# Products of gathered rows taken earlier and in smaller lots in the expert search of a two-part transformer block, with fewer early weight chunks

## The chip, the cores and the metric

The kernel runs on 1 core of one Trainium2 chip. The metric is device time in microseconds (us) of one execution, median over the runs shown.

## The reference, cut to what matters

One sequence of 256 tokens with 1024 features goes through a first block (block attention, difference attention, then an expert layer) and a second block (two attention mixers). The change lies in the expert layer:

```python
def chunk_fn(xc):                                   # 128 tokens at a time
    q = (xc @ w_query).reshape(C, PEER_HEADS, 2, PEER_HALF)
    sc = jnp.einsum('thpd,hpnd->thpn', q, sub_keys)
    top_s, top_i = lax.top_k(sc, PEER_TOPK)         # 16 of 128, for 8 heads x 2 halves
    cand_s = top_s[:, :, 0, :, None] + top_s[:, :, 1, None, :]
    best_s, best_pos = lax.top_k(cand_s, PEER_TOPK) # 16 pairs a head: 128 slots a token
    experts = jnp.take_along_axis(cand_i, best_pos, axis=-1)
    gates = jax.nn.softmax(best_s, axis=-1)
    u, vv = expert_down[experts], expert_up[experts]
    act = jax.nn.gelu(jnp.einsum('cd,chkd->chk', xc, u), approximate=False)
    return jnp.einsum('chk,chkd->cd', gates * act, vv)
```

There are 16,384 experts, each with a row of 1024 numbers in `expert_down` and one in `expert_up`.

## The kernel before, in words

The function select_phase does everything of the expert layer up to the weights of the experts; experts_phase then multiplies these with `expert_up`. The 256 tokens are two tiles of 128, called t = 0 and t = 1 here, and the two are treated differently:

- **Tile 1** is multiplied with all of `expert_down`. Its 128 chunks of 128 experts (512 KB each) are loaded by SyncE (Chunks.load, L1314 and L1317), TensorE multiplies one (Chunks.project, L1331, 16 matmul records a chunk), and ScalarE takes the gelu of four chunks at a time (Chunks.gelu, L1342).
- **Tile 0** gathers only the rows it chose. For each of the 128 slots GpSimd issues one indirect DMA of one row a token (512 KB, L1459) and VectorE multiplies and sums that buffer in one instruction (the function dots, L1682). There are GATHERS = 12 gather buffers; gather s waits until product s - 12 is done (semaphore `dotted`).

Both kinds of load use the same 16 DMA engines, through two queues: SyncE's and GpSimd's.

The order in which the stages come, on the engines:

1. **Queries and scores.** 16 half heads hp. For each, SyncE loads a 576 KB piece of weights (`route`, L1426, into ring buffer hp % 4 once the scores of hp - 4 are out), ScalarE and GpSimd split it (L1542, L1450), TensorE makes the queries (L245 to L247) and the scores (L1487). Behind each of the 12 loads of this stage SyncE puts one load of an early chunk; the other early chunks go out before the first of them. EARLY = 18 chunks are early: they lie where table and gather buffers lie later, 12 of them in the 12 gather buffers, so the first 12 gathers wait for TensorE to be through with them (`projected`). The later chunks use a ring of 6 buffers.
2. **The searches** on VectorE. halves(t, h) finds the 16 best scores of both halves of one head (L1611, L1614, L1616), pairs(t, n) the best sums of four heads (L1631 and the same top-16 rows), indices(t, n) their numbers (L1646 to L1664), choose(n) hands 64 slots of tile 0 to GpSimd (L1675). TensorE works through AHEAD = 56 chunks meanwhile. ScalarE puts the exp of the gates (L1571) behind the gelu of 48 chunks and ahead of the rest.
3. **The slot transposes** (L1493) and then **the table of tile 1**, 16 groups of 8 tokens: VectorE makes one one-hot factor (onehots, L1703), ScalarE the other (equal, L1553 and L1556), TensorE multiplies them (spread, L1505), ScalarE copies one part out (L1581), VectorE merges the other (merge, L1716). Between the groups TensorE has the chunks up to 80, and VectorE DOTS_GROUP = 3 products a group, 17 times.
4. **The rest**: the other chunks up to 120 on TensorE, the other products and the joins (join, L1724) on VectorE, all paced so that the last product and the last of these chunks end together.
5. **The table of tile 0**, 16 groups, which needs all products of tile 0; then the expert phase.

The constants `DOTS_...` say how many products VectorE has done where: 4 after the second choose, 1 after each of the last four halves of tile 1, 3 after each indices of tile 1, 2 before the slot transposes: 16 before the table, 67 behind it.

```python
for n in range(2):
    for h in range(4 * n, 4 * n + 4):
        halves(0, h)
        if n == 0:
            halves(1, h)
    pairs(0, n); indices(0, n); choose(n)
```

Of the kernel before, what the change touches and what calls it, by code (L numbers as in the profile page):

```python
# [32 lines left out]
NT = SEQ // P  # L33
# [8 lines left out]
HEADS_P = 8  # L42
TOPK = 16
SLOTS = HEADS_P * TOPK
# [2 lines left out]
FIRST_FREE = 4  # L47
UP_RING = 4
GATHERS = 12
EARLY = GATHERS + 6  # L50
EARLY_ROWS = 2
BEFORE = 48
AHEAD = 56
BESIDE = 32
TAIL = 8
WAITING = BESIDE // 4
DOTS_FIRST, DOTS_HALVES, DOTS_INDEX, DOTS_TURN, DOTS_GROUP = 4, 1, 3, 2, 3
RECTANGLES = ((0, 0, 1, 16), (16, 1, 4, 8), (40, 4, 8, 4), (56, 8, 16, 1))
PAIRS = 64
BY_SCALAR = (0, 1, 2, 5, 8, 11, 14)  # L60
# [1284 lines left out]
def select_phase(nc, d, hT, hT_at, whole, sbt, raw, landed_q, table, table_at, h_row, chunks, gather_in, up_in):  # L1345
# [3 lines left out]
    HP = 2 * HEADS_P  # L1349
    NW = 4  # L1350
    Q = 8
    GROUPS = P // Q
    BATCH = 4
    BATCHES = GROUPS // BATCH
    begun = DOTS_FIRST + 4 * DOTS_HALVES + 2 * DOTS_INDEX + DOTS_TURN + DOTS_GROUP * (GROUPS + 1)
    last_groups = (NKEYS - TAIL - BEFORE - BESIDE) // 4
    beside = [AHEAD + (BEFORE + BESIDE - AHEAD) * g // GROUPS for g in range(GROUPS + 1)]
    COARSE = P // FINE
# [28 lines left out]
    with ExitStack() as c:  # L1387
# [28 lines left out]
        @block.sync  # L1416
        def _(sp):
            sp.dma_start(h_row[:], d["ffn_row"].broadcast_to([P, D])).then_inc(gain_in, 16)
            sp.dma_start(starts[:], d["c_starts"]).then_inc(starts_in, 16)
            sp.dma_start(mask_word[:], d["c_masks"]).then_inc(masks_in, 16)  # L1420
            first = EARLY - (HP - NW)
            for n in range(first):
                chunks.load(sp, n)
            for hp in range(NW, HP):
                sp.wait_ge(s_ready, hp - NW + 1)
                sp.dma_start(raw[hp % NW][:], weights[hp]).then_inc(landed_q[hp % NW], 16)  # L1426
                chunks.load(sp, first + hp - NW)
            for n in range(EARLY, NKEYS):
                if n < EARLY + RING - FIRST_FREE:
                    pass  # L1430
                elif n < EARLY + RING:
                    sp.wait_ge(s_ready, HP - NW + chunks.buffer(n) + 1)
                else:
                    sp.wait_ge(chunks.projected, n - RING + 1)
                paced = n // 4 - (BEFORE + BESIDE) // 4 - 1
                if paced > 0:
                    sp.wait_ge(dotted, begun + (SLOTS - begun) * min(paced, last_groups) // last_groups)
                chunks.load(sp, n)
            for n in range(UP_RING):
                sp.wait_ge(chunks.projected, chunks.last_in(n) + 1)  # L1440
                sp.dma_start(raw[n][:, 0:KD, :].rearrange("p k c -> p (k c)"), d["up"][n]).then_inc(up_in[n], 16)

        @block.gpsimd
        def _(pool):
            for hp in range(2, HP):
                b = hp % NW
                for h in range(2):
                    k = slice(KD // 2 * h, KD // 2 * (h + 1))
                    pool.wait_ge(w_highs, hp * 2 + (h - 3))
                    pool.tensor_tensor(w_low[b % 2][:, k], raw[b][:, k], w_high[b % 2][:, k].bitcast(F32),  # L1450
                                       ALU.subtract).then_inc(w_lows, 1)
            for s in range(SLOTS):
                if s % PART == 0:
                    pool.wait_ge(chosen, s // PART + 1)
                if s < GATHERS:
                    pool.wait_ge(chunks.projected, EARLY_ROWS + s + 1)
                else:
                    pool.wait_ge(dotted, s - GATHERS + 1)
                pool.indirect_dma_start(gathered[s % GATHERS], None, d["down_rows"],  # L1459
                                        bass.IndirectOffsetOnAxis(ap=expert[:, s:s + 1], axis=0)).then_inc(gather_in[s % GATHERS], 16)  # L1460
# [143 lines left out]
        def _(dve):  # L1604
# [14 lines left out]
            def halves(t, h):  # L1619

                dve.wait_ge(s_saved, 2 * h + 2)
                top16([(saved[:, hp, t * P:(t + 1) * P], rest[:, hp % 2, :], lambda r, hp=hp: topv[:, t, hp, 8 * r:8 * r + 8],
                        lambda r, hp=hp: topu[:, t, hp, 8 * r:8 * r + 8]) for hp in (2 * h, 2 * h + 1)])

            def pairs(t, n):

                first, second = [topv[:, t, n * HEADS_P + half:(n + 1) * HEADS_P:2, :] for half in range(2)]
                four = HEADS_P // 2
                for at, lo, hi, width in RECTANGLES:
                    shape = [P, four, hi - lo, width]  # L1630
                    dve.tensor_tensor(cand[:, :, at:at + (hi - lo) * width].rearrange("p i (a b) -> p i a b", b=width),  # L1631
                                      first[:, :, lo:hi].unsqueeze(3).broadcast_to(shape),
                                      second[:, :, 0:width].unsqueeze(2).broadcast_to(shape), ALU.add)
                dve.drain()
                top16([(cand[:, i], crest[:, i], lambda r, at=(n * four + i) * TOPK: bestv[:, t, at + 8 * r:at + 8 * r + 8],
                        lambda r, at=(n * four + i) * TOPK: pos[:, t, at + 8 * r:at + 8 * r + 8]) for i in range(four)])
# [37 lines left out]
                dve.drain()  # L1674
                dve.tensor_copy(expert[:, at], number[:, at]).then_inc(chosen, 1)  # L1675

            def dots(lo, hi):

                for s in range(lo, hi):
                    b = s % GATHERS  # L1680
                    dve.wait_ge(gather_in[b], s // GATHERS * 16 + 16)
                    dve.tensor_tensor_reduce(gathered[b], gathered[b], h_row[:], 1.0, 0.0, ALU.mult, ALU.add, u[:, s:s + 1]).then_inc(dotted, 1)  # L1682

            def digit(t, n, part):

# [41 lines left out]
            dve.scalar_tensor_tensor(h_row[:], x[:, 0, :], sbt["root"][:, 0:1], h_row[:], ALU.mult, ALU.mult)  # L1727
            dve.wait_ge(starts_in, 16)
            dve.wait_ge(masks_in, 16)
            for n in range(2):  # L1730
                for h in range(4 * n, 4 * n + 4):
                    halves(0, h)
                    if n == 0:
                        halves(1, h)
                pairs(0, n)
                indices(0, n)
                choose(n)
            at = DOTS_FIRST
            dots(0, at)
            for n in range(2):  # L1740
                for h in range(4 * n, 4 * n + 4):
                    if n == 1:
                        halves(1, h)
                        dots(at, at + DOTS_HALVES)
                        at += DOTS_HALVES
                pairs(1, n)
                indices(1, n)
                dots(at, at + DOTS_INDEX)
                at += DOTS_INDEX
            for t in range(NT):  # L1750
                v = bestv[:, t, :].rearrange("p (h k) -> p h k", k=TOPK)
                last = dve.tensor_tensor(gate[:, t, :].rearrange("p (h k) -> p h k", k=TOPK), v,
# [16 lines left out]
                v = gate[:, t, :].rearrange("p (h k) -> p h k", k=TOPK)  # L1769
                last = dve.tensor_tensor(v, v, ginv[:, t, :].unsqueeze(2).broadcast_to([P, HEADS_P, TOPK]), ALU.mult)  # L1770
            last.then_inc(cols_ready, 1)
            dots(at, at + DOTS_TURN)
            at += DOTS_TURN
            dve.wait_ge(cols_turned, 2)
            dve.tensor_copy(slotT[:, 1], slots[:, 1])
            dve.tensor_copy(slotT[:, 0, 0:3], slots[:, 0, 0:3])
# [3 lines left out]
            for g in range(GROUPS + 1):  # L1780
                if g < GROUPS:
                    onehots(1, g)
                if g > 0:
                    merge(g - 1)
                dots(at, at + DOTS_GROUP)
                at += DOTS_GROUP
            first, last = BEFORE // 4, (NKEYS - TAIL) // 4
            middle = (BEFORE + BESIDE) // 4
            for g in range(first, middle):
                join(g, late_gelu[g - first])  # L1790
            left = SLOTS - at
            for n, g in enumerate(range(middle, last)):
                dots(at + left * n // (last - middle), at + left * (n + 1) // (last - middle))
                join(g, late_gelu[(g - first) % WAITING])
            dve.drain().then_inc(dots_done, 1)
            for part in range(2):
# [121 lines left out]
def build(nc, d, out):  # L1918
    ctx = ExitStack()
    with ctx:  # L1920
# [29 lines left out]
        with ExitStack() as c0:  # L1950
# [71 lines left out]
            with ExitStack() as c:  # L2022
                table_at = -(-nc.sbuf_base // 32) * 32
                table = sb("table", [P, NT, NKEYS, P], c=c)
                h_row = sb("h_row", [P, D], c=c)
                up_in = [sem(f"up_in{b}") for b in range(UP_RING)]
                with ExitStack() as c2:
                    in_ring, in_rows = [[table[:, t].rearrange("p n t -> p (n t)")[:, b * D:(b + 1) * D].rearrange("p (k e) -> p k e", k=KD)
                                         for b in range((GATHERS, EARLY - GATHERS)[t])] for t in range(NT)]
                    early = in_rows[0:EARLY_ROWS] + in_ring + in_rows[EARLY_ROWS:]  # L2030
                    chunks = Chunks(nc, c2, plain_u, d["downT"], whole, raw, early)
                    select_phase(nc, d, hT, hT_at, whole, sbt, raw, landed_q, table, table_at, h_row, chunks, gather_in, up_in)
                c1.close()
                cleared = experts_phase(nc, d["up"], table, hT, x, whole, raw, up_in, sbt["sums"], sbt["ident"])
# [82 lines left out]
```

## Time and profile before

| | before |
|---|---|
| median of 3 runs | 1519.17 us (1518.54 to 1522.5) |
| the profiled execution: its own time | 1524.2 us |
| the profiled execution: span from first to last instruction | 1522.4 us |
| TensorE busy | 1409.8 us (93%) |
| VectorE busy | 993.1 us (65%) |
| ScalarE busy | 636.8 us (42%) |
| GpSimd busy | 205.5 us (13%) |
| read from HBM | 304.73 MB |

Busy time is an average over stages with different limits: the stage that the change touches lies between 183 us and 627 us of the span. In the rows, PE is TensorE, DVE VectorE, ACT ScalarE, POOL GpSimd and SPq the DMA-issuing queue of SyncE. "table" in a row can be any of the things that lie in the table's memory: scores, search scratch, gather buffers, early chunks.

### The profile page before, as it was taken

The page shows a single profiled execution, that of the slowest core. Times are in us where ns is not written, and L with a number is a line of the kernel's source. Part 1 is how long each engine was busy: PE and PEld are TensorE (multiplying, and loading weights), DVE is VectorE, ACT ScalarE, POOL GpSimd, SP SyncE. Part 2 cuts the span into 40 slices and gives each one's busy share as a digit, 9 for nine tenths or more (in the row PEclk, how much of TensorE's full clock was granted, in tenths as well). Part 3 has the DMA queues.
Part 4 walks back from the last instruction along what each step waited for, and adds up shares of the span by engine and source line. Part 5 has one row for each costly group of instructions (what it writes and reads, how often), then busy time and mean ns, then how long its engine had stood idle before and what let it go on. Part 6 is the DMA issues. An engine that isn't in the chain of part 4 may idle for free. (4 is left out here: it accounts for less than half of the span.)

```text
span 1522.4 us, 24797 instructions
## 1 busy us (share of the span) xinstructions
PE 1409.8 (93%) x8327; PEld 1212.7 (80%) x8327; DVE 993.1 (65%) x2325; ACT 636.8 (42%) x1256; POOL 205.5 (13%) x170
## 2 busy tenths in 40 slices
PE   7998989997896758999999999999999999989998
PEld 4665689997796658777777777789999999659994
DVE  4666569977996567566666666665555555256761
ACT  2433242017750005433333333356665665326651
POOL 0000164325876420000000000000000000000000
PEclk9999999999997988999999999999999999999999
DMA  8330187898999992365656556485554443236630
GB/s 299 133 137 1 46 333 263 314 386 307 404 409 409 409 403 85 99 191 181 191 188 185 192 182 191 138 249 176 178 153 153 152 152 111 91 89 193 183 90 28
DMA packets 145527, 307.17 MB, mean 202 GB/s; under 512 B 39968, under 2 KB 89632, under 8 KB 143904
## 3 DMA queue, kind: packets, MB, share of 16 engines
q1 hardware_dynamic: 127008, 238.93, 46.9%
q0 software_dynamic: 18432, 67.12, 11.5%
q8 instruction: 50, 0.82, 0.2%
q14 instruction: 37, 0.30, 0.1%
HBM read 304.73 MB, written 1.29 MB: 201 GB/s over the span
## 5 line engine op out<-in xcount | busy, mean ns | idle before, releaser
L1331 PE MATMUL plain_u<-whole,ring 128*128 128x128 f32 x1760 | 218.3, 285 | 34.6 <-DMA ring<-in_downT 34.6
L1331 PEld LDWEIGHTS plain_u<-whole,ring 128*128 128x128 f32 x1760 | 210.8, 200 | 40.2 <-DMA ring<-in_downT 40.0
L1882 ACT ACTIVATE hT_high<-ring 128x1024 fp32r<-128x1024 f32 x128 | 135.8, 1061 | 224.8 <-PE experts_acc L247 223.7
L245 PE MATMUL experts_acc<-hT_high,experts_wh 128*128 128x512 f32 x512 | 204.5, 399 | 1.5 <-DVE hT_low L1898 1.5
L246 PE MATMUL experts_acc<-hT_low,experts_wh 128*128 128x512 f32 x512 | 203.2, 397 | 0.0
L247 PE MATMUL experts_acc<-hT_high,experts_wl 128*128 128x512 f32 x512 | 203.2, 397 | 0.0
L1682 DVE CUSTOM_DVE_ANT_0 table<-table,h_row 128x1024 f32<-128x1024 f32 x128 | 152.3, 1223 | 45.1 <-DMA table<-in_down_rows,select_expert 41.6
L1459 POOL DMA_INDIRECT table<-in_down_rows,select_expert x128 | 161.6, 1262 | 145.1 <-DVE select_u L1682 101.4
L1898 DVE TENSOR_TENSOR hT_low<-ring,hT_high 128x1024 fp32r<-128x1024 f32 x128 | 156.9, 1226 | 27.4 <-ACT hT_high L1882 27.4
L245 PE MATMUL mix_a_pj<-mix_a_wh,hT_high 128*128 128x384 f32 x368 | 129.1, 351 | 0.0
L245 PEld LDWEIGHTS experts_acc<-hT_high,experts_wh 128*128 128x128 f32 x512 | 96.6, 189 | 35.2 <-issue 7.5
L247 PE MATMUL mix_a_pj<-mix_a_wh,hT_low 128*128 128x384 f32 x368 | 123.5, 336 | 0.0
L246 PE MATMUL mix_a_pj<-mix_a_wl,hT_high 128*128 128x384 f32 x368 | 123.4, 335 | 0.0
L247 PEld LDWEIGHTS experts_acc<-hT_high,experts_wl 128*128 128x128 f32 x512 | 96.8, 189 | 23.3
L246 PEld LDWEIGHTS experts_acc<-hT_low,experts_wh 128*128 128x128 f32 x512 | 96.9, 189 | 17.8
L1342 ACT ACTIVATE table<-plain_u 128x512 f32<-128x512 f32 x30 | 17.9, 597 | 203.3 <-PE plain_u L1331 189.6
L675 PE MATMUL block_pj<-block_w_raw,whole 128*128 128x384 f32 x256 | 91.1, 487 | 1.0 <-PEq L1196 1.0
L624 DVE TENSOR_TENSOR mix_a_wl<-mix_raw,mix_a_wh 128x1536 fp32r<-128x1536 f32 x46 | 80.5, 1756 | 14.3 <-ACT mix_a_wh L855 12.5
L1894 DVE CAST experts_wh<-table 128x256 fp32r (+1 forms) x128 | 37.8, 295 | 75.1 <-PE experts_acc L247 74.8
L246 PEld LDWEIGHTS mix_a_pj<-mix_a_wl,hT_high 128*128 128x128 f32 x368 | 69.4, 188 | 0.0
L245 PEld LDWEIGHTS mix_a_pj<-mix_a_wh,hT_high 128*128 128x128 f32 x368 | 69.3, 188 | 0.0
L247 PEld LDWEIGHTS mix_a_pj<-mix_a_wh,hT_low 128*128 128x128 f32 x368 | 69.1, 188 | 0.0
(393 smaller groups left out, 2601.9 us busy)
## 6 DMA issues: line engine op xcount, KB each, us to landing
ring<-in_up SPq DMA_DIRECT2D x128, 512.0 KB, 3.5
ring<-in_downT SPq DMA_DIRECT2D x110, 512.0 KB
mix_raw<-in_wa SPq DMA_DIRECT2D x46, 768.0 KB, 6.2
block_w_raw<-in_w SPq DMA_DIRECT2D x16, 768.0 KB, 6.2
mix_raw<-in_wb SPq DMA_DIRECT2D x16, 768.0 KB, 6.7
ring<-in_route SPq DMA_DIRECT2D x16, 576.0 KB, 5.2
table<-in_downT SPq DMA_DIRECT2D x18, 512.0 KB, 6.0
wo<-in_wo SPq DMA_DIRECT2D x4, 1024.0 KB, 7.9
```

What stands on the lines that cost most here:

```text
L245: pe.matmul(out, lhs[0], rhs[0], start=start, stop=False, skip_group_check=True)
L246: pe.matmul(out, lhs[0], rhs[1], start=False, stop=False, skip_group_check=True)
L247: return pe.matmul(out, lhs[1], rhs[0], start=False, stop=stop, skip_group_check=True)
L624: eng.tensor_tensor(wl[w][:, k, c], pieces.raw[w][:, k, c], wh[w][:, k, c].bitcast(F32), ALU.subtract).then_inc(lows, 1)
L675: mm = pe.matmul(dst[:, 0:3 * P], hT[:, k, chunks[i][1] * P:(chunks[i][1] + 1) * P], pieces.raw[b][:, k, :], start=k == 0, stop=k == KD - ...
L1331: mm = pe.matmul(self.u[g % 2][:, i * P:(i + 1) * P], rows[:, k, :], self.h[:, k, P:SEQ], start=k == 0, stop=k == KD - 1, skip_group_check ...
L1342: act.activation(into, self.u[g % 2][:], ACT.Gelu).then_inc(self.taken, 1)
L1459: pool.indirect_dma_start(gathered[s % GATHERS], None, d["down_rows"], bass.IndirectOffsetOnAxis(ap=expert[:, s:s + 1], axis=0)).then_inc( ...
L1682: dve.tensor_tensor_reduce(gathered[b], gathered[b], h_row[:], 1.0, 0.0, ALU.mult, ALU.add, u[:, s:s + 1]).then_inc(dotted, 1)
L1882: act.activation(uh[b % 2], raw_u[b], ACT.Copy).then_inc(u_high, 1)
L1894: dve.tensor_copy(wh[b % 2][:], table[:, :, n, :])
L1898: dve.tensor_tensor(ul[b % 2], raw_u[b], uh[b % 2].bitcast(F32), ALU.subtract).then_inc(u_low, 1)
```

## The change

The first four gather buffers no longer hold early chunks, so there are 14 early chunks instead of 18; the first four gathers wait for `chosen` alone, and gathers 4 to 11 each for the chunk in their buffer. Products now begin inside the first search: 2 after each of the halves of heads 5, 6 and 7 of tile 0, 5 after each of three indices, 3 after each pairs of tile 1, 2 after each of the last four halves of tile 1, 3 before the slot transposes: 38 before the table instead of 16. In the table a group has 1 and 2 products in turn instead of 3: 25 instead of 51, so 63 are done behind the table instead of 67, and 65 instead of 61 remain. TensorE has 60 chunks before the slot transposes and 20 between the groups of the table, instead of 56 and 24.

```diff
-EARLY = GATHERS + 6
+FREE = 4
+EARLY = GATHERS - FREE + 6
-AHEAD = 56
+AHEAD = 60
-DOTS_FIRST, DOTS_HALVES, DOTS_INDEX, DOTS_TURN, DOTS_GROUP = 4, 1, 3, 2, 3
+DOTS_FIRST, DOTS_LISTS, DOTS_PAIRS, DOTS_INDEX, DOTS_TURN = 2, 2, 3, 5, 3
...
-            first = EARLY - (HP - NW)
+            first = max(0, EARLY - (HP - NW))
...
-                if s < GATHERS:
-                    pool.wait_ge(chunks.projected, EARLY_ROWS + s + 1)
-                else:
+                if FREE <= s < GATHERS:
+                    pool.wait_ge(chunks.projected, EARLY_ROWS + s - FREE + 1)
+                elif s >= GATHERS:
                     pool.wait_ge(dotted, s - GATHERS + 1)
...
+            for h in range(4):
+                halves(0, h)
+                halves(1, h)
+            pairs(0, 0)
+            indices(0, 0)
+            choose(0)
+            at = 0
+            for h in range(4, HEADS_P):
+                halves(0, h)
+                if h > 4:
+                    at = dots(at, DOTS_FIRST)
+            pairs(0, 1)
+            indices(0, 1)
+            choose(1)
+            at = dots(at, DOTS_INDEX)
+            pairs(1, 0)
+            at = dots(at, DOTS_PAIRS)
+            indices(1, 0)
+            at = dots(at, DOTS_INDEX)
+            for h in range(4, HEADS_P):
+                halves(1, h)
+                at = dots(at, DOTS_LISTS)
+            pairs(1, 1)
+            at = dots(at, DOTS_PAIRS)
+            indices(1, 1)
+            at = dots(at, DOTS_INDEX)
...
-            dots(at, at + DOTS_TURN)
-            at += DOTS_TURN
+            at = dots(at, DOTS_TURN)
...
-                dots(at, at + DOTS_GROUP)
-                at += DOTS_GROUP
+                at = dots(at, 1 + g % 2)
```

SyncE's queue at the start of the stage: `table<-in_downT` is an early chunk, `ring<-in_route` a weight piece. Before:

```order
L1418 DMA h_row<-in_ffn_row 128x1024
L1419 DMA select_starts<-in_c_starts 128x17
L1420 DMA select_mask_word<-in_c_masks 128x1
L1314 DMA table<-in_downT 128x1024 x6
L1426 DMA ring<-in_route 128x1152
```

Now:

```order
L1420 DMA h_row<-in_ffn_row 128x1024
L1421 DMA select_starts<-in_c_starts 128x17
L1422 DMA select_mask_word<-in_c_masks 128x1
L1316 DMA table<-in_downT 128x1024 x2
L1428 DMA ring<-in_route 128x1152
```

Two early chunks stand ahead of the first weight piece of this queue instead of six.

VectorE in the halves of heads 5 and 6 of tile 0, between the first choose and the second (an ISA row with `table,select_u<-table,h_row` is a product; the ISA row behind it reads its sum). Before:

```order
L1611 MAX table<-table 128x8 x2
L1614 MAX_INDEX table<-table 128x8 x2
L1611 MAX table<-table 128x8 x2
L1614 MAX_INDEX table<-table 128x8
L1616 MATCH_REPLACE table<-table 128x128
```

Now:

```order
L1614 MAX table<-table 128x8 x2
L1617 MAX_INDEX table<-table 128x8 x2
L1685 ISA table,select_u<-table,h_row 128x1024
L1685 ISA select_u 128x1
L1685 ISA table,select_u<-table,h_row 128x1024
L1685 ISA select_u 128x1
L1614 MAX table<-table 128x8 x2
```

Two products stand where head 6 followed on head 5.

VectorE in two groups of the table of tile 1. Before:

```order
L1703 TENSOR_TENSOR select_a_one_1992<-select_coarse_of,select_fine_of 128x1024
L1716 TENSOR_TENSOR table<-table,select_four 128x48x8
L1682 ISA table,select_u<-table,h_row 128x1024
L1682 ISA select_u 128x1
L1682 ISA table,select_u<-table,h_row 128x1024
L1682 ISA select_u 128x1
L1682 ISA table,select_u<-table,h_row 128x1024
L1682 ISA select_u 128x1
L1703 TENSOR_TENSOR select_a_one_1991<-select_coarse_of,select_fine_of 128x1024
```

Now:

```order
L1707 TENSOR_TENSOR select_a_one_1992<-select_coarse_of,select_fine_of 128x1024
L1720 TENSOR_TENSOR table<-table,select_four 128x48x8
L1685 ISA table,select_u<-table,h_row 128x1024
L1685 ISA select_u 128x1
L1685 ISA table,select_u<-table,h_row 128x1024
L1685 ISA select_u 128x1
L1707 TENSOR_TENSOR select_a_one_1991<-select_coarse_of,select_fine_of 128x1024
```

One product fewer stands between these two one-hot factors; the group behind has one product where it had three.

## Rows read from the trace of the kernel before

**Rows 1.** The page's DMA issues: loads of ring chunks, with KB each
```profile
ring<-in_downT SPq DMA_DIRECT2D x110, 512.0 KB
```

**Rows 2.** Stretches: busy PE, PEld, DVE, ACT, POOL; clock; DMA share; GB/s
```profile
244.00:264.00 20.00, 20.00 (x179) 20.00 (x180) 18.24 (x111) 3.19 (x5) 7.67 (x8) 1.00 0.66 221
264.00:352.00 88.00, 82.80 (x730) 81.72 (x728) 68.77 (x225) 12.54 (x23) 23.73 (x20) 1.00 0.94 354
352.00:384.00 32.00, 25.63 (x201) 25.09 (x202) 29.00 (x47) 29.30 (x71) 22.26 (x14) 0.90 0.80 283
384.00:444.00 60.00, 53.81 (x460) 53.04 (x459) 59.63 (x96) 39.43 (x93) 49.65 (x34) 0.97 1.03 409
444.00:571.00 127.00, 85.17 (x623) 80.23 (x622) 82.87 (x139) 15.06 (x33) 58.29 (x53) 0.87 1.02 407
```

**Rows 3.** VectorE in order of time (start us, us): a late product, the last join
```profile
471.44 1.23 DVE L1682 CUSTOM_DVE_ANT_0 table<-table,h_row 128x1024 f32<-128x1024 f32 x1 [1.32 <-DMA table<-in_down_rows,select_expert]
...
572.42 0.69 DVE L1724 TENSOR_TENSOR table<-table 128x512 f32<-128x512 f32 x1
```

**Rows 4.** Queries in order of time, TensorE then ScalarE; the stretch's clock
```profile
190.82 0.36 PE L245 MATMUL select_four<-hT_high,select_w_high 128*128 128x256 f32 x1
...
193.75 0.61 PE L1487 MATMUL select_four<-ring,table 128*128 128x128 f32 x4
199.92 0.55 PE L245 MATMUL select_four<-hT_high,select_w_high 128*128 128x256 f32 x1 [5.57 <-POOL select_w_low L1450]
...
204.97 0.61 PE L1487 MATMUL select_four<-ring,table 128*128 128x128 f32 x4
...
197.80 1.15 ACT L1542 ACTIVATE select_w_high<-ring 128x512 fp32r<-128x512 f32 x2 [6.32 <-DMA ring<-in_route]
...
198.00:204.00 6.00, 4.08 (x19) 4.11 (x20) 0.00 (x0) 2.65 (x6) 5.02 (x4) 0.50 0.88 352
```

**Rows 5.** TensorE in order of time: the first chunks, 16 records each
```profile
244.48 17.70 PE L1331 MATMUL plain_u<-whole,table 128*128 128x128 f32 x157
```

**Rows 6.** VectorE in order of time: first choose, products, end of the searches
```profile
245.54 0.20 DVE L1675 CAST select_expert<-table 128x64 uint32<-128x64 f32 x1
...
326.97 1.22 DVE L1682 CUSTOM_DVE_ANT_0 table<-table,h_row 128x1024 f32<-128x1024 f32 x1
328.11 0.49 DVE L1752 TENSOR_TENSOR select_gate<-select_bestv 128x128 f32<-128x128 f32 x2
```

**Rows 7.** ScalarE in order of time: the exp between two gelus
```profile
333.77 1.28 ACT L1571 ACT_TABLE_LOAD   x1
...
335.50 1.28 ACT L1342 ACT_TABLE_LOAD   x1
```

**Rows 8.** From the slot transposes to the end of the table
```profile
347.38 0.49 PE L1493 MATMUL select_slots<-ident,select_columns_of 128*128 128x128 f32 x3
...
351.49 1.23 DVE L1703 TENSOR_TENSOR select_a_one<-select_coarse_of,select_fine_of 128x1024 f32<-128x1024 f32 x1
...
444.13 5.02 DVE L1724 TENSOR_TENSOR table<-table 128x512 f32<-128x512 f32 x8
```

**Rows 9.** Groups of instructions from 351 to 444 us; ScalarE's start to start
```profile
L1703 DVE TENSOR_TENSOR select_a_one<-select_coarse_of,select_fine_of 128x1024 f32<-128x1024 f32 x16 | 19.6, 1224 | 0.4
L1716 DVE TENSOR_TENSOR table<-table,select_four 128x384 f32<-128x384 f32 x16 | 8.8, 550 | 2.8 <-ACT table L1581 2.8
...
360.90 2.44 ACT L1553 ACTIVATE select_a_two<-iota,select_columns_of 128x128 f32<-128x128 f32 x8
364.47 0.68 ACT L1581 ACTIVATE table<-select_four 128x640 f32<-128x640 f32 x1
365.06 2.44 ACT L1553 ACTIVATE select_a_two<-iota,select_columns_of 128x128 f32<-128x128 f32 x8
```

**Rows 10.** Gather issues (POOL): ns min/median/max, from 246 to 272 and 351 to 444
```profile
L1459 POOL DMA_INDIRECT table<-in_down_rows,select_expert x12: 939/940/1547, 250.9 to 270.0; - x12
...
L1459 POOL DMA_INDIRECT table<-in_down_rows,select_expert x48: 937/1492/1993, 354.7 to 443.0; - x48
```

More of the change, by code:

```diff
@@ L56 @@
 WAITING = BESIDE // 4
-DOTS_FIRST, DOTS_HALVES, DOTS_INDEX, DOTS_TURN, DOTS_GROUP = 4, 1, 3, 2, 3
+DOTS_FIRST, DOTS_LISTS, DOTS_PAIRS, DOTS_INDEX, DOTS_TURN = 2, 2, 3, 5, 3
+DOTS_SEARCH = 3 * DOTS_FIRST + 2 * DOTS_PAIRS + 4 * DOTS_LISTS + 3 * DOTS_INDEX + DOTS_TURN
 RECTANGLES = ((0, 0, 1, 16), (16, 1, 4, 8), (40, 4, 8, 4), (56, 8, 16, 1))
@@ L1354, in select_phase @@
     BATCHES = GROUPS // BATCH
-    begun = DOTS_FIRST + 4 * DOTS_HALVES + 2 * DOTS_INDEX + DOTS_TURN + DOTS_GROUP * (GROUPS + 1)
+    begun = DOTS_SEARCH + sum(1 + g % 2 for g in range(GROUPS + 1))
     last_groups = (NKEYS - TAIL - BEFORE - BESIDE) // 4
@@ L1426, in _ @@
                 sp.dma_start(raw[hp % NW][:], weights[hp]).then_inc(landed_q[hp % NW], 16)
-                chunks.load(sp, first + hp - NW)
+                if first + hp - NW < EARLY:
+                    chunks.load(sp, first + hp - NW)
             for n in range(EARLY, NKEYS):
@@ L1675, in choose, with dots @@
                 dve.tensor_copy(expert[:, at], number[:, at]).then_inc(chosen, 1)
-            def dots(lo, hi):
-                for s in range(lo, hi):
+            def dots(lo, n):
+                for s in range(lo, lo + n):
                     b = s % GATHERS
@@ L1682, in dots @@
                     dve.tensor_tensor_reduce(gathered[b], gathered[b], h_row[:], 1.0, 0.0, ALU.mult, ALU.add, u[:, s:s + 1]).then_inc(dotted, 1)
+                return lo + n
             def digit(t, n, part):
@@ L1729, in _ @@
             dve.wait_ge(masks_in, 16)
[L1730 to L1749, printed above, removed]
+            for h in range(4):
[24 more added lines that the diff above has]
+            at = dots(at, DOTS_INDEX)
             for t in range(NT):
@@ L1790, in _ @@
                 join(g, late_gelu[g - first])
-            left = SLOTS - at
+            left = SLOTS - begun
             for n, g in enumerate(range(middle, last)):
-                dots(at + left * n // (last - middle), at + left * (n + 1) // (last - middle))
+                at = dots(at, left * (n + 1) // (last - middle) - left * n // (last - middle))
                 join(g, late_gelu[(g - first) % WAITING])
@@ L2028, in build @@
                     in_ring, in_rows = [[table[:, t].rearrange("p n t -> p (n t)")[:, b * D:(b + 1) * D].rearrange("p (k e) -> p k e", k=KD)
-                                         for b in range((GATHERS, EARLY - GATHERS)[t])] for t in range(NT)]
+                                         for b in (range(FREE, GATHERS), range(EARLY - GATHERS + FREE))[t]] for t in range(NT)]
                     early = in_rows[0:EARLY_ROWS] + in_ring + in_rows[EARLY_ROWS:]
```

## The prediction

> **What bounds the kernel now.** I read the stretches of the expert search first. From 384 us to 571 us the DMA engines move 409 and 407 GB/s without a gap [rows 2]; a transfer of 512 KB [rows 1], a chunk or a gather, is 524,288 bytes, so it costs 1.28 us at that rate. Then VectorE in order of time: behind the table a product takes 1.23 us and is preceded by 1.32 us in which VectorE waits for its gather [rows 3], 2.55 us in all, two transfers: one gather and one chunk in turn. The last join begins at 572.42, the products end there, and the table of tile 0 and the expert phase follow at a fixed distance. So the end of this stage is a sum of transfers plus the time in which the DMA engines stood idle. Idle time, by 1 - rate/409 [rows 2]: 9.2 us from 244 to 264 (221 GB/s), 11.8 from 264 to 352 (354), 9.9 from 352 to 384 (283), 0.6 behind that: 31.5 us. The whole question is how much of it the change uses, and how much it makes anew.
>
> **Part 1, four early chunks fewer: the queries start 7.4 us earlier.** In the queries TensorE waits 5.57 us until 199.92, and ScalarE 6.32 us until 197.80 for a weight piece [rows 4]. That piece stands in SyncE's queue behind six early chunks; now it stands behind two. Four transfers are 5.1 us, so it lands near 192.7 and TensorE goes on at about 194.7 instead of 199.92. The pause also halves the clock: granted 0.50 from 198 to 204, and the half head that follows takes 5.05 us (199.92 to 204.97) where one at full clock took 2.93 (190.82 to 193.75) [rows 4]. A pause of about 0.4 us should not do this. Together 5.2 + 2.1 = 7.3, and I take 7.4 for all that follows in the queries. The chunks then start at 244.48 - 7.4 = 237.1 [rows 5], and the first choose, at 245.7 [rows 6], at 238.3. Against it: 20 chunks instead of 24 are in by then, so four transfers, 5.1 us of DMA, are added behind this point.
>
> **Part 2, products in the searches.** VectorE has 35 products there instead of 14. One costs 1.14 us from start to start [rows 6], and VectorE is nearly always busy there (68.8 of 88 us, with its pause before the table in it [rows 2]). The searches end at 328.1 - 7.4 + 21 x 1.14 = 344.7 us [rows 6]. In return, 50 gathers are issued by the slot transposes (38 + 12) instead of 28. The first four start at once and go into a stretch where the DMA idles.
>
> **Part 3, the start of the table.** Three things can be last.
> - ScalarE: the exp of the gates waits for the end of the searches and is queued ahead of the gelu of chunks 48 to 51, on which chunk 56 waits for its PSUM bank. It and its two table loads take 3.0 us [rows 7], a gelu 0.6: chunk 56 is free at about 349, four chunks of 1.8 us [rows 5] end at 356.
> - VectorE: about 352, with three products.
> - The DMA: by the end of chunk 59, about 42 more chunks and 48 gathers have to land after 237.1: 90 x 1.28 = 115.4 us. To this comes idle time. At least 5 us (no gather before 238.3, and only chunks between the first 18 gathers and the second choose), at most the 21 us that the kernel before shows from 244 to 352 [rows 2]. I take 9, near the low end, because 18 gathers instead of 12 are ready to go in the first stretch. With 3 us for the last landing and its product: 364.5, from 360 to 376.
>
> The DMA is last. From the transposes to the first one-hot factor it was 351.5 - 347.4 = 4.1 us [rows 8], so the table starts at 368.5 instead of 351.5: 17 us later.
>
> **Part 4, the table itself.** It took 444.1 - 351.5 = 92.6 us [rows 8], VectorE's time: 19.6 + 8.8 us of factors and merges [rows 9] and 51 products of 1.14. With 25 products VectorE needs some 60 us, and ScalarE is next: a one-hot factor takes 3.57 us from start to start, a copy 0.59 [rows 9], and five gelus in all 0.16 a group, 4.32 x 16 = 69 us. TensorE has a spread of about 1.8 us and 1.25 chunks a group, 4.0 us. With 5.5 us at the ends I take 74.5 (70 if the last groups go at TensorE's pace, 80 if it waits for chunks). The table ends at 443.0 instead of 444.1. Of the 26 products it lost, 21 had been paid for in part 2: that is why so little is left.
>
> **Part 5, the rest.** Before, 127 us at 407 GB/s were 98.6 transfers [rows 2], in 128.3 us (444.1 to 572.4). Now 53 gathers beyond the 75 issued and some 42 chunks are left when all buffers are full. In the table the new kernel wants 25 gathers and 20 chunks in about 75 us, 58 us of DMA, so the buffers do fill: I count three transfers in flight, and three chunks that load after the last gather: 95. That is 3.6 transfers fewer, -4.6 us, although four products more remain: 123.7 us. The products end at 443.0 + 123.7 = 566.7 instead of 572.4: **-5.7 us**. The same by the other account: start -7.4, four chunks +5.1, idle 28 us instead of 31.5: -5.8. About 17 of these 28 us lie in the table, where 9.9 lay before.
>
> Everything else hides: GpSimd issues a gather in 0.94 us beside the halves and 1.49 in the median beside the table [rows 10], plus some 0.3 between two, always under the 2.55 us of a pair of transfers. The rest of the program is the same. The sum is against the profiled execution (1524.2 us, span 1522.4), which is 5 us above the median of 1519.17; the difference is taken off the median: **1513.5 us**.
>
> **The rivals.**
> - *The idle time only moves (within 0.3%).* If the DMA loses 14 us instead of 9 before the table, or the table takes 79 us, 5 us go: 571.7, 1518.5 us. For it: in the stretch from 264 to 352 the DMA was below its rate although chunks were always wanted [rows 2], and the table must idle. If the pause in the queries stayed, because the weight pieces are late for another reason, the result would be +1.7 us, 1521: the part of the change that would then not do what it says. Together 0.36.
> - *Gathers are issued too slowly beside the products (slower).* GpSimd's issue beside products was stretched up to 1.99 us [rows 10]. There are now lots of five products, behind which five gathers are issued. It decides when the table starts behind 379: 32 gathers issued from 264 us on would then have to take over 3.3 us each, gap included. At 3.4 us they take 109 us, the last lands near 375, and the table starts near 381: 381 + 74.5 + 123.7 = 579.2, +6.8 us, 1526. Against it: 1.49 is the median even with three products a group, and 1.99 the longest. The Trainium skill, page "SBUF — State Buffer", section "Who interferes with whom", has VectorE and GpSimd lock a pair of SBUF ports against each other for a whole instruction, and the same page gives a GpSimd-issued DMA of some 620 ns about 3100 ns beside a VectorE copy; by that figure this rival would be the case, but no row here comes near it. The same late start would come if gathers were served first and TensorE waited for chunks. 0.14.
> - *The table starts at ScalarE's bound (much faster).* If the DMA idles 1 us only, the start is 360.1, the end of the table 434.6, the last product 558.3: -14 us, 1505. Against it: the stretch between the first 18 gathers and the second choose has only chunks to load. 0.12.
>
> **How the numbers follow.** The forecast as worked out, between 4.6 and 10 us faster, has 0.38. A measurement of this kernel can tell about 0.3%, 4.6 us, from no change. Faster by more than that: 0.38 + 0.12 = 0.50; within it: 0.36; slower: 0.14. The bounds of parts 3 and 4 are -8 and +12 us for the start, -4.5 and +5.5 for the table; they are not all met at once. The range from 1503 to 1523 takes in the start at 360 with a short table, and the start near 375 with a longer one, and leaves out most of the slower rival.
>
> **What would show it.** The wait of 5.57 us ahead of the fifth half head gone, full clock there and the first chunk at 237; the end of the searches at 345; the slot transposes near 364; one-hot factors at ScalarE's 4.3 us a group; the DMA at 409 GB/s from about 271 to 364, below it in the table (some 330), and at 409 again to the end; the last join at 567. It is wrong if the transposes come behind 375, if groups of the table take over 5 us, or if products before the table wait for gathers.

## The result and the profile after

| | before | changed kernel |
|---|---|---|
| median | 1520.61 us (20 runs, 1515.68 to 1528.34) | **1526.21 us** (20 runs, 1519.05 to 1530.51) |
| ratio | | 1.0031, 95% interval 1.0018 to 1.0045 |
| profiled execution, time and span | 1524.2, 1522.4 | 1521.15, 1519.4 |

The forecast was 1513.5 us (1503 to 1523), most likely faster. The changed kernel is not faster, and by its median 0.3% slower. Twice more, against other runs of the kernel before, it had ratios of 1.0009 and 1.0027 (below).

The stretches of the changed kernel that answer to [rows 2]; columns: busy time of PE, PEld, DVE, ACT and POOL, then granted clock, DMA share and GB/s.
```profile
244.00:264.00 20.00, 19.59 (x174) 19.25 (x173) 18.81 (x90) 1.79 (x3) 14.07 (x14) 1.00 0.92 326
264.00:352.00 88.00, 75.89 (x621) 71.12 (x621) 82.71 (x250) 8.95 (x13) 41.90 (x32) 1.00 1.02 398
352.00:384.00 32.00, 22.60 (x167) 21.25 (x167) 10.98 (x17) 15.98 (x40) 4.29 (x3) 0.89 0.75 279
384.00:444.00 60.00, 57.51 (x507) 56.94 (x508) 52.61 (x81) 52.69 (x127) 31.48 (x22) 1.00 0.94 329
444.00:571.00 127.00, 87.75 (x647) 83.15 (x645) 86.36 (x144) 16.91 (x38) 65.39 (x55) 0.88 1.01 398
```
By 1 - rate/409 DMA is idle for 4.1, 2.4, 10.2, 11.7 and 3.4 us in these stretches, 31.8 us in all; in the kernel before it was 31.5 [rows 2]. Up to 352 us the change gained 14.5 us of DMA time. From 352 us on, mostly beside the table, it lost the same again (14.8 us).

TensorE in order of time: the end of the fourth half head and the start of the fifth, the first chunks (answers to [rows 4, 5]), the last two chunks before the transposes, and the transposes (answer to [rows 8]).
```profile
193.67 0.61 PE L1490 MATMUL select_four<-ring,table 128*128 128x128 f32 x4
194.69 0.36 PE L247 MATMUL select_four<-hT_high,select_w_high 128*128 128x256 f32 x1 [0.42 <-POOL select_w_low L1453]
...
235.88 25.42 PE L1333 MATMUL plain_u<-whole,table 128*128 128x128 f32 x224
...
362.23 2.05 PE L1333 MATMUL plain_u<-whole,ring 128*128 128x128 f32 x16 [0.50 <-DMA ring<-in_downT]
364.80 2.05 PE L1333 MATMUL plain_u<-whole,ring 128*128 128x128 f32 x16 [0.52 <-DMA ring<-in_downT]
366.69 0.49 PE L1496 MATMUL select_slots<-ident,select_columns_of 128*128 128x128 f32 x3
```
The wait of 5.57 us is now 0.42, and the chunks begin 8.6 us earlier. The other end is at 362 us: one chunk per 2.57 us, each with a wait of 0.5 us for its landing. From 352 to 367 us the two queues share DMA nearly evenly, 3.68 MB for chunks and 3.25 MB for gathers, so about one gather lands between two chunks. The transposes come 19.3 us later than in [rows 8].

VectorE in order of time: the end of the searches, its next wait, the first one-hot factor, the first joins, the last products and the last join (answers to [rows 3, 6, 8]).
```profile
344.04 0.49 DVE L1762 TENSOR_TENSOR select_gate<-select_bestv 128x128 f32<-128x128 f32 x2
...
367.65 0.69 DVE L1784 COPY select_columns_of<-select_slots 128x512 f32<-128x512 f32 x1 [16.79 <-PE select_slots L1496]
...
370.80 1.23 DVE L1707 TENSOR_TENSOR select_a_one<-select_coarse_of,select_fine_of 128x1024 f32<-128x1024 f32 x1
...
443.56 4.92 DVE L1728 TENSOR_TENSOR table<-table 128x512 f32<-128x512 f32 x8
...
567.80 1.23 DVE L1685 CUSTOM_DVE_ANT_0 table<-table,h_row 128x1024 f32<-128x1024 f32 x1 [1.32 <-DMA table<-in_down_rows,select_expert]
...
572.87 0.69 DVE L1728 TENSOR_TENSOR table<-table 128x512 f32<-128x512 f32 x1
```
VectorE has made its last product before the table, the 38th, at 350.9 us and then waits 16.79 us for the transposes. In that time no gather buffer comes free, and the table starts with all of them full. The last join is at 572.87 us where it was at 572.42 [rows 3].

### The profile page after: what moved, and what is told of

The parts are those of the page before. It is cut to its first block and busy times, and to the rows that moved or that the text cites. A ratio compares the mean times of both kernels' runs of the same rounds, so it can differ in the third digit from the quotient of the medians.

```text
span 1519.4 us, 24796 instructions
## 1 busy us (share of the span) xinstructions
PE 1409.4 (93%) x8327; PEld 1208.3 (80%) x8327; DVE 992.2 (65%) x2325; ACT 635.2 (42%) x1256; POOL 206.8 (14%) x170
## 5 line engine op out<-in xcount | busy, mean ns | idle before, releaser
L1333 PE MATMUL plain_u<-whole,ring 128*128 128x128 f32 x1824 | 232.1, 286 | 46.2 <-DMA ring<-in_downT 42.6
L1333 PEld LDWEIGHTS plain_u<-whole,ring 128*128 128x128 f32 x1824 | 219.8, 199 | 56.5 <-DMA ring<-in_downT 52.2
L626 DVE TENSOR_TENSOR mix_a_wl<-mix_raw,mix_a_wh 128x1536 fp32r<-128x1536 f32 x46 | 80.5, 1756 | 14.4 <-ACT mix_a_wh L857 12.7
```

What stands on the lines that cost most here:

```text
L626: eng.tensor_tensor(wl[w][:, k, c], pieces.raw[w][:, k, c], wh[w][:, k, c].bitcast(F32), ALU.subtract).then_inc(lows, 1)
L1333: mm = pe.matmul(self.u[g % 2][:, i * P:(i + 1) * P], rows[:, k, :], self.h[:, k, P:SEQ], start=k == 0, stop=k == KD - 1, skip_group_check ...
```

## The experiments

For each run I give the ratio of its median to that of the kernel before on the same chip, and the last join (L1728, 0.69 us) of its profile. Two theories stood at the start. A: how late the stage of the gathered rows ends is decided by the time in which DMA stood idle, wherever that is. B: the stage isn't what differs. Each expectation says what A and B mean for that run.

### The three parts apart

**Only fewer early chunks.**
```
 # the kernel before
+FREE = 4
-EARLY = GATHERS + 6
+EARLY = GATHERS - FREE + 6
...
-                if s < GATHERS:
-                    pool.wait_ge(chunks.projected, EARLY_ROWS + s + 1)
+                if FREE <= s < GATHERS:
+                    pool.wait_ge(chunks.projected, EARLY_ROWS + s - FREE + 1)
```


> The kernel before with the first part of the change alone: 4 gather buffers free of early chunks, 14 early chunks; products and the 56 chunks as before. Theory A: the 7.4 us by which the first chunk products come earlier are kept as far as the queues stay busy: last join near 566.5 us, 1514.5 us (-6). Theory B (the freed buffers change nothing in the end): 1520.5 us within 1.5.

Measured: 1515.63 us, ratio 0.9959 (0.9943 to 0.9975), last join at 566.48. This one part gives all that I forecast for the whole change: 5.9 us in the stage (4.8 to 6.5 against the three profiles of the kernel before that are shown below).

**That, and 60 chunks up to the transposes** (`AHEAD = 60`), products as before.

> The kernel before with 4 free gather buffers and with 60 chunks up to the slot transposes; products as before. Theory A (the 4 chunks hold the table back by the time that TensorE waits for them): slot transposes 5 to 7 us later than with 56 (341.7 us), last join 3 to 5 us later than 566.5 us, 1519.5 us. Theory B (4 chunks more or less before the transposes are made up beside the table): 1515.6 us within 1.

Measured: 1518.43 us, 0.9998 (0.9982 to 1.0014), transposes at 348.71, last join at 570.99. Four chunks more put the transposes 7.0 us later (341.66 without them) and cost 4.5 us in the stage: theory A.

**The changed kernel with 56 chunks** (`AHEAD = 56`), twice.

> The changed kernel with 56 chunks up to the slot transposes in place of 60, products as changed. Theory A (TensorE waits for chunks one per 2.56 us at the end of the searches, and these 4 chunks hold the table back): the transposes come 8 to 10 us earlier, near 357.5 us, DMA carries the same in the table with more products to be made behind it, last join near 564 us, 1517 us (-9 against the changed kernel). Theory B (the stage is bound by its bytes whatever the order): within 1.5 us of the changed kernel.

> The changed kernel with 56 chunks before the transposes, for a profile at an undisturbed clock. Theory A (TensorE is served one chunk per 2.56 us there, so 4 chunks are 10 us of the 19 by which the table starts later): transposes near 357 us, searches' end unchanged at 345 us, table ends near 437 us, last join near 566 us, the median 4 to 5 us under the changed kernel's. Theory B (the searches' end sets the transposes): transposes within 2 us of 366 us.

Measured: 1518.37 us, 0.9970 (0.9951 to 0.9989), and 1517.02 us, 0.9973 (0.9961 to 0.9986). The profiled execution of the first had a mean clock of 0.929 and isn't read. In the second the transposes are at 356.28, the last join at 565.87:
```profile
264.00:352.00 88.00, 75.31 (x619) 70.81 (x618) 83.48 (x251) 8.95 (x13) 42.20 (x32) 1.00 1.02 400
352.00:384.00 32.00, 26.37 (x208) 25.84 (x209) 20.43 (x31) 25.65 (x65) 10.22 (x8) 0.89 0.88 323
384.00:444.00 60.00, 60.00 (x538) 59.90 (x537) 51.08 (x79) 49.91 (x121) 28.80 (x20) 1.00 0.99 359
...
565.87 0.69 DVE L1728 TENSOR_TENSOR table<-table 128x512 f32<-128x512 f32 x1
```
From 264 to 352 it is the same program at the same rate. The table comes 10.4 us earlier, which is four chunks at 2.57 us, and of these the stage keeps 7.0 (6.8 against the changed kernel on the same chip, below). With products as before the four chunks delay the transposes by 7.0 us only: in that run the last gather before the transposes was issued at 334.6, and TensorE takes the last chunks without a wait, at 1.8 us each.

The run with 56 chunks differs from the one with only fewer early chunks in the products alone. Its last join is 0.6 us earlier, its ratio 0.9970 and 0.9973 instead of 0.9959, with intervals that overlap: moving the products had no effect that these runs can tell.

**The changed kernel itself,** three times more, the last beside the run with 56 chunks.

> The changed kernel once more, nothing edited. Theory A (the loss is in the stage of the gathered rows: the traffic that DMA did not carry at the searches' end and beside the table is owed behind it): a profile again shows the last join near 572.9 us, and a run that takes 1526 us shows it later, by as much as the run is longer. Theory B (the stage is equal, and the time is lost elsewhere, in the clock or in the experts' phase): the last join stays within 1 us of 572.4 us and the experts' phase is longer than in the profile of before. Time by both: 1526 us, +0.3%.

> The changed kernel, nothing edited, for a third profile, since its runs spread over 15 us at nearly one clock. Theory A (the spread is in the stage of the gathered rows, in the stretch from 289 to 366 us where TensorE takes each chunk as it lands, or in the one behind the table): a profile longer by n us has its last join later by about n. Theory B (the spread is in the experts' phase): last join 572 to 573 us whatever the time.

> The changed kernel once more beside these two, so that all are compared on one chip. Theory A: 1523 to 1526 us in the median, last join at 572 to 573 us in the profile.

Measured: 1523.08 us, 1.0009 (0.9991 to 1.0027), last join 572.05; 1519.16 us (one run), 572.49; 1523.45 us, 1.0027 (1.0011 to 1.0043), 572.66. In one comparison on one chip, 56 chunks in place of 60 are worth 6.4 us of the median, and the intervals of the two ratios don't touch (1.0011 to 1.0043, 0.9961 to 0.9986).

### The products beside the table

**Two products with every group,** first with 60 chunks, then with 56.
```
 # the changed kernel
-    begun = DOTS_SEARCH + sum(1 + g % 2 for g in range(GROUPS + 1))
+    begun = DOTS_SEARCH + 2 * (GROUPS + 1)
...
-                at = dots(at, 1 + g % 2)
+                at = dots(at, 2)
```


> The changed kernel (60 chunks, its products beside the searches) with two products with every group of the table in place of one and two by turns; that alone. Theory A (what the change lost is DMA's idle time beside the table, 9.7 to 11.9 us of it from 384 to 444 us): idle there under 3 us, table no more than 2 us longer, last join near 561 us, 1513.5 us. Theory B (beside the table all gathers and chunks that are needed are there, and the 17 us for which the table comes later decide): last join at 572 us, 1523 to 1526 us.

> As the run with 56 chunks, and two products with every group of the table in place of one and two by turns (72 products by the table's end in place of 63). Theory A (beside the table DMA is idle for want of freed gather buffers): idle time of DMA beside the table falls from 11.7 us to under 4, last join near 555 us, 1508 us (-18 against the changed kernel), as long as VectorE's 9 more products, 10 us in all, hide below ScalarE's 4.3 us a group. Theory B (VectorE is not free there): the table gets 8 to 10 us longer and the time stays within 2 us of the run with 56 chunks.

Measured: with 60 chunks 1515.62 us, 0.9959 (0.9944 to 0.9974), last join 568.80; with 56 chunks 1506.38 us, 0.9897 (0.9868 to 0.9926), last join 556.18. By the medians they are faster by 7.8 and 12.0 us than the kernels with one and two by turns in the same comparison (1523.45 and 1518.37), as theory A has it. The profiles bear this out for the second (9.7 us in the stage, 565.87 - 556.18), and only in part for the first. That one gained 3.9 us in the stage (572.66 - 568.80) where theory A had 11; the other 3.9 us by which its profiled execution is shorter lie behind the last join (last section). From 384 to 444 us its DMA idle time was 8.1 us, not under 3, and its table took 76.8 us, not at most 74.8. The transposes came at 372.06, 5.4 us later than in the changed kernel, an edit behind them notwithstanding: DMA was below its rate long before, with the clock down for part of the stretch:
```profile
264.00:272.00 8.00, 7.12 (x36) 6.42 (x36) 6.95 (x11) 0.60 (x1) 0.50 (x1) 0.58 0.78 298
```

**Three with every group, as before, and fewer beside the second search.** The constants are `DOTS_FIRST, DOTS_LISTS, DOTS_PAIRS, DOTS_INDEX, DOTS_TURN = 2, 1, 0, 5, 4`, 56 chunks, `dots(at, 3)`.

> 56 chunks up to the transposes, fewer products beside the second search (31 and 4 before the transposes in place of 38 in all), and 3 with every group of the table as in the kernel before: 31 + 51 = 82 products by the table's end in place of 63. Theory A (DMA's idle time is the loss): searches end near 338 us, DMA beside the table idle under 2 us, last join near 550 us, 1500 us (-6 against two products a group, -20 against before). Theory B (VectorE becomes the bound of the table at 3 products a group, 4.9 us a group in place of 4.3): table longer by 8 us, time as with two a group, 1506 us.

Measured: **1505.53 us, 0.9895 (0.9871 to 0.9919)**, last join 553.96:
```profile
264.00:352.00 88.00, 78.51 (x679) 76.30 (x678) 80.19 (x258) 12.43 (x23) 32.74 (x27) 0.99 1.01 392
352.00:384.00 32.00, 25.76 (x206) 25.22 (x207) 29.02 (x47) 28.76 (x70) 22.52 (x15) 0.92 0.99 375
384.00:444.00 60.00, 53.31 (x451) 52.17 (x451) 58.72 (x96) 38.78 (x91) 49.11 (x34) 0.97 1.03 409
...
346.80 0.49 PE L1496 MATMUL select_slots<-ident,select_columns_of 128*128 128x128 f32 x3
...
553.96 0.69 DVE L1728 TENSOR_TENSOR table<-table 128x512 f32<-128x512 f32 x1
```
The expectation miscounts: these constants give 25 + 4 = 29 products before the table and 80 by its end (the trace has as many), not 82. Theory A's 550 us and 1500 us were missed by 4 and 5.5 us. DMA is at 409 GB/s beside the table, and near it before. The table takes 93.8 us (350.9 to 444.7) in place of 72.8, as theory B feared, and that costs nothing, since it starts 20 us earlier. This kernel and the one with 56 chunks and two products a group are 1% faster than both that were to be compared. Their intervals overlap: which of the two is better isn't told.

**One product behind each of the 8 joins at the table's end.**
```
             for g in range(first, middle):
                 join(g, late_gelu[g - first])
+                at = dots(at, 1)
-            left = SLOTS - begun
+            left = SLOTS - begun - BESIDE // 4
```


> The changed kernel with one product behind each of the 8 joins at the table's end, in place of all 8 joins first. Theory A (VectorE frees no gather buffer for 4.9 us there, and the gathers' queue runs dry): DMA from 440 to 460 us at 405 GB/s or more in place of 0.89 of it, last join 2 to 3 us earlier, 1520.5 us. Theory B (gathers and chunks that could not go there are made up behind): 1523 to 1526 us, last join within 0.7 us of 572.9.

Measured: 1522.31 us, 1.0018 (1.0000 to 1.0036), last join 570.95. From 440 to 460 us the rate went from 367 to 384 GB/s, not to 405:
```profile
440.00:460.00 20.00, 18.57 (x160) 17.80 (x158) 19.77 (x36) 12.40 (x31) 16.65 (x12) 1.00 1.00 384
```
The gap behind the joins is small at most: the last join is 1.9 us earlier than in the first profile and 1.1 earlier than in the lowest of the changed kernel's, and the ratio lies between the changed kernel's own three (1.0009 to 1.0031). It is not where the change failed.

### One account for all

From 236 us to the last join each kernel moves the same data: 123.0 to 123.7 MB in all the profiles below, 301 to 302 us at 409 GB/s. The rest of the time is idle DMA, worked out as above for five stretches. That the sum follows the last join is arithmetic, within the 1.7 us that 0.7 MB take; what the table adds is where each kernel lost its time:

| kernel | 236-300 | 300-352 | 352-384 | 384-444 | 444-join | sum | last join |
|---|---|---|---|---|---|---|---|
| before | 20.3 | 2.4 | 9.9 | 0.0 | 1.9 | 34.5 | 572.42 |
| fewer early chunks | 14.6 | 7.1 | 4.6 | 0.0 | 1.8 | 28.1 | 566.48 |
| and 60 chunks | 14.6 | 2.7 | 12.3 | 0.7 | 2.5 | 32.7 | 570.99 |
| all three parts | 8.8 | 0.0 | 10.2 | 11.7 | 5.4 | 36.0 | 572.87 |
| with 56 chunks | 9.4 | 0.1 | 6.7 | 7.3 | 5.7 | 29.2 | 565.87 |
| with 2 a group | 12.8 | 0.0 | 7.5 | 8.1 | 3.4 | 31.8 | 568.80 |
| 56, 2 a group | 9.9 | 0.1 | 5.0 | 1.8 | 2.5 | 19.2 | 556.18 |
| 56, 3 a group | 10.0 | 2.3 | 2.7 | 0.0 | 1.1 | 16.0 | 553.96 |

### Where the rest of the median is

The stages of the two first profiles end 0.45 us apart, the medians differ by 5.6 us. Three more profiles were taken for that.

> The kernel before, nothing edited, for a second profile of it. Theory A (the change's loss is in the stage, and the first profile of before ended it late for that kernel): last join at 568 to 571 us, 1519 to 1521 us. Theory B (stages equal): last join at 572 to 573 us, and the difference of the medians lies behind it.

> The kernel before, nothing edited, for a third profile: as the second. Theory A: last join at 568 to 571 us. Theory B: at 572 to 573 us.

> The changed kernel, nothing edited, beside the two profiles of before on one chip. Both theories: last join at 572 to 573 us; theory A also allows later, up to 578 us, in an execution of 1525 us or more.

Measured: the kernel before against itself 1.0004 (0.9992 to 1.0016), last joins 571.26 and 572.94. The changed kernel on that chip: 1525.31 us, last join **577.35**. So the stage of before ends within 1.7 us in three profiles, and that of the changed kernel within 0.8 us in four and 4.5 us later in a fifth. VectorE in that fifth profile:
```profile
248.04 1.23 DVE L1685 CUSTOM_DVE_ANT_0 table<-table,h_row 128x1024 f32<-128x1024 f32 x1 [0.67 <-issue]
...
266.77 0.23 DVE L1652 CAST table<-table 128x128 f32<-128x128 uint32 x1 [1.97 <-issue]
...
276.18 0.20 DVE L1678 CAST select_expert<-table 128x64 uint32<-128x64 f32 x1
```
and the same copy in the first profile:
```profile
270.86 0.20 DVE L1678 CAST select_expert<-table 128x64 uint32<-128x64 f32 x1
```
VectorE stood still for 0.67, 1.97 and two times under 0.4 us without a reason that the profile shows, and was 5.3 us late at this second choose, with the first one 2.3 us late. Everything behind it was late too: 354 GB/s from 264 to 300 us, searches' end at 349.36, transposes at 370.64, last join by 4.5 us. The four other profiles had the second choose at 270.9 to 274.0 us and all the same last join, which suggests some slack that was used up here. Between 236 and 276 us such gaps are also in the profile with two products a group (1.33 and 0.90 us) and, with 0.53, in one more of the changed kernel; the three of the kernel before have none. That is an association and not a cause shown: why the engine stands there, and how much of the 2 to 6 us between the medians it is, stays open. The profiles may also have missed what the longer executions spend: all five profiled executions of the changed kernel took 1519.16 to 1525.31 us, less than its median of 1526.21 in the first comparison, where others took up to 1530.51.

## Why the prediction was wrong

The forecast failed in size at part 5, the stretch behind the table, and in kind by not asking what the 60 chunks cost.

- **Part 1** was right: wait gone, full clock, first chunk at 235.9 (237.1 forecast), first choose at 237.6 (238.3; 239.0 to 240.0 in the four later profiles). Alone it gave 5.9 us.
- **Part 2** was right: searches end at 344.04 (344.7).
- **Part 3** was right in which resource is last, DMA: transposes 366.69 (364.5), first factor 370.80 (368.5). The 2.2 us are the small miss of this term, made of two that nearly cancel: by its rate of 384 GB/s from 237.10 to 366.69 DMA moved 94.9 transfers and not 90 (+6.3 us), and was idle for 7.9 us, not 9 and 3 for the last landing (-4.1).
- **Part 4** was right: the table takes 72.8 us (74.5) at ScalarE's pace and ends at 443.56 (443.0).
- **Part 5** failed: "53 gathers beyond the 75 issued and some 42 chunks are left when all buffers are full ... 95", in 123.7 us. It took 129.31 us:
```profile
443.56:572.87 129.31, 88.19 (x651) 83.59 (x649) 88.50 (x150) 16.91 (x38) 65.83 (x55) 0.88 0.99 392
```
 392 GB/s for 129.31 us are 96.7 transfers, 1.7 more than counted: 2.2 us. And 129.31 x (1 - 392/409) = 5.4 us are idle. The forecast held less: I took 3.6 transfers off the 128.3 us of before, and with them kept that stretch's idle time, 1.9 us by its rate over the whole of it:
```profile
444.13:572.42 128.29, 85.04 (x622) 80.10 (x621) 83.89 (x140) 14.93 (x33) 58.16 (x53) 0.87 1.01 403
```
 So 3.5 us more are idle, and with the 2.2 this is the miss of 5.6 within rounding. By the view of the changed kernel 1.3 of the 5.4 us lie before 460 us, around the joins, and 3.8 in the last 21 us, when little is left to load:
```profile
443.56:460.00 16.44, 15.47 (x139) 15.28 (x137) 15.24 (x28) 11.86 (x30) 10.08 (x9) 1.00 1.00 377
...
552.00:572.87 20.87, 9.89 (x64) 9.70 (x64) 11.62 (x20) 0.60 (x1) 0.00 (x0) 0.66 0.84 334
```
 I had tested the full buffers by whether they could fill in 75 us, not whether DMA was busy when they emptied again.
- The account beside it ("idle 28 us instead of 31.5") had the same hole: 9 of these us stood before the table, 17 in it, and so only 2 behind it. From 352 to 444 us there were 21.9, nearly all of them in the table, and 5.4 behind.
- Behind these terms stands what I didn't weigh: parts with opposite signs. I treated the change as one, and "the DMA is last" in part 3 never asked what fewer than 60 chunks would give. Measured in the stage, fewer early chunks are -5.9 us and the other two parts together +6.4. The four chunks more before the transposes cost 4.5 (products as before) or 7.0 (products as changed, 572.87 - 565.87). What is left for the products is +1.9 with 60 chunks and -0.6 with 56, too little to tell from the spread between profiles.
- The rival "the idle time only moves" came true in the profiles by its outcome: 571.7 us was its last join, 572.87 is measured, with an idle sum of 31.8 against 31.5 us. Its conditions did not: DMA lost 7.9 us before the transposes, not 14, and the table took 72.8 us, not 79. That the number fits is luck. It had 0.36, together with the pause in the queries. Its time, 1518.5 us, was still too low for the median.
- The slow issue of gathers did not come: with 33 gathers from 263 to 352 us, GpSimd's longest was 1.99 us and its median 1.05, and it waited for products for 39.5 us of that stretch:
```profile
L1462 POOL DMA_INDIRECT table<-in_down_rows,select_expert x33: 933/1050/1991, 263.1 to 352.1; - x33
```
 The 3100 ns that the Trainium skill, page "SBUF — State Buffer", section "A bandwidth-pool intuition that's wrong (but worth ruling out)", gives for such an issue beside a VectorE copy were not seen beside products. The forecast also gave the lock of a port pair without its limit: the section "Who interferes with whom" has the other engine wait for a whole instruction where VectorE runs in a two-port mode, and no run here tells which mode a product runs in.
- The measured median is 12.7 us above the forecast, and the stage explains 6.2 of them (572.87 instead of 566.7). Another 1.4 us is the median of the kernel before, 1520.61 over 20 runs instead of the 1519.17 that I started from. The other 5.1 us stay open, as said above.
- The times were set against a single profiled execution whose span had 3 us more than others for a reason outside the stage (below). For a forecast of 0.4% such a difference matters.

## What to carry to other kernels

When a stage's data is fixed and DMA carries it at its full rate, its length is that data plus DMA's idle time. List the idle time by stretch, and ask of each part of a change alone whether it removes some or only moves it. Work that frees buffers is worth most where DMA would otherwise find them all full: here, with 56 chunks, 3 products in every group of the table and fewer before it (VectorE busy for 58.7 of 60 us) ended the stage 11.9 us earlier than 1 and 2 in turn, though that table was 18 us shorter (75.4 instead of 93.8 us). And measure the parts apart: the four chunks more lost what the fewer early chunks had won.

## What was not expected of the hardware

From the last join to the end of the span the program is the same, yet that time fell in two groups over the 15 profiles with an ordinary clock. The stretch just behind the start of the experts' phase tells them apart, in the kernel before and in the changed one:
```profile
626.00:632.00 6.00, 3.90 (x13) 3.19 (x14) 3.96 (x7) 2.00 (x2) 0.00 (x0) 0.66 0.28 84
```
```profile
626.00:632.00 6.00, 4.39 (x21) 3.64 (x22) 4.06 (x8) 2.43 (x3) 0.00 (x0) 1.00 0.52 167
```
Where the granted clock was at its half level for some 7 us there (for before, 6.8 us by its shares of 0.66 from 626 to 632 and 0.83 from 632 to 640), the tail took 947.8 to 951.4 us (six profiles; before 950.0, the changed kernel 948.1 and 948.5); with 3.4 us or none it took 944.6 to 946.5 us (nine more; before 945.8 and 946.5, the changed kernel 946.5, 944.9 and 946.2). Both kernels were seen in both groups, so some 3 us of a single profile's span go with it, and not with an edit here. Why the clock falls there in some executions and not in others is not shown.
